# High parts of the MLP weights in a float32 encoder made by a converting GpSimd transfer instead of a ScalarE copy

## The chip, the cores and the metric

The kernel runs on one core of a Trainium2 chip. Its engines are PE (TensorE, the matmuls), PEld (the loads of weights into TensorE), DVE (VectorE), ACT (ScalarE), POOL (GpSimd) and SP (SyncE, which here only issues transfers). The metric is the device time of one execution in microseconds. Lower is better.

## The reference

An encoder of two layers runs over 512 tokens of width 1024. Layer 0 mixes tokens by 2-D neighbourhood attention, layer 1 by sliding-window attention, and each is followed by the same squared-ReLU MLP. Everything is float32.

```python
def squared_relu_mlp(h, w_in, w_out):
    u = jnp.square(jax.nn.relu(jnp.einsum('bsd,df->bsf', h, w_in)))
    return jnp.einsum('bsf,fd->bsd', u, w_out)

def reference(x, mix_norm, mlp_norm, final_norm, na_w_qkv, na_rpb, na_w_o,
              swa_w_qkv, swa_sinks, swa_w_o, t5_rel_table, mlp_w_in, mlp_w_out):
    for i in range(DEPTH):
        j = i // N_MIXERS
        h = rms_norm(x, mix_norm[i])
        if i % N_MIXERS == 0:
            x = x + neighbourhood_attention(h, na_w_qkv[j], na_rpb[j], na_w_o[j])
        else:
            x = x + sliding_window_gqa(h, swa_w_qkv[j], swa_sinks[j], t5_rel_table, swa_w_o[j])
        h = rms_norm(x, mlp_norm[i])
        x = x + squared_relu_mlp(h, mlp_w_in[i], mlp_w_out[i])
    return rms_norm(x, final_norm)
```

`D_MODEL` is 1024, the hidden width `D_FF` is 4096, and both MLPs are of this size.

## The kernel before

**Two parts for each number.** TensorE multiplies in the format float32r, which keeps fewer bits than float32. So every operand is split into a high part (the value rounded to float32r) and a low part (the value less its high part, rounded likewise). One product of float32 tiles is then three matmuls (L364 to L366): high by high, high by low and low by high, all added up in PSUM.

**Weights as a stream of chunks.** The host lays all weights out as 180 chunks of 128x1024 float32, 512 KB each. A chunk is eight 128x128 blocks and so 24 matmuls. Chunks 32 to 95 belong to the first MLP and 116 to 179 to the second. In each MLP the hidden width is done in two halves. A half has 16 chunks of `w_in` (the "hidden" loop, one chunk for each tile of 128 hidden features) and then 16 of `w_out` (the "down" loop, two chunks for each of the 8 output tiles).

**A ring of two.** `w_raw`, `w_hi` and `w_lo` each hold two chunks, even ones in slot 0 and odd ones in slot 1. A chunk `c` passes through four hands:

1. SP loads `w_raw` (L248) once the subtraction of chunk `c-2` is done (`w_split`).
2. ACT copies `w_raw` to `w_hi`, which rounds it (L721). It waits for PE to be done with chunk `c-2` (`w_used`), since that one's high part is in the same slot, and for the load.
3. DVE subtracts, `w_lo = w_raw - w_hi` (L967), and raises `w_split`.
4. PE waits for `w_split`, does the 24 matmuls and raises `w_used`.

Nothing schedules this. Each engine has a program written out in order, and only semaphores couple them. In the hidden loop, PE's end of chunk `f` lets DVE scale the result out of PSUM (`scale_tile`, L995) and then subtract for chunk `f+2`. ACT squares (L753) and rounds (L757) the scaled tile, and DVE makes its low part (`tile_low`, L1005). In the down loop DVE adds the result to the residual `x` (`add_to_x`, L1107) between two subtractions.

**GpSimd** builds the attention biases: it issues the transfers of bias rows (L292, L314) and adds a mask (L304). During the MLPs it has nothing to do.

**The last output tile** (`last_group`) goes through chunks 178 and 179 twice, once for each half of the tokens, so its first pass over chunk 178 takes half as long as that of another chunk.

Of the kernel before, what the change touches and what calls it, by code (L numbers as in the profile page):

```python
# [32 lines left out]
HALF = FF // 2 // P  # L33
# [20 lines left out]
CH_NA, CH_NAO, CH_MLP0 = 0, 24, 32  # L54
CH_SW, CH_SWO, CH_MLP1 = 96, 108, 116
CHUNKS = 180
GR_NA, GR_NAO, GR_MLP0, GR_SW, GR_SWO, GR_MLP1 = 0, 24, 32, 80, 92, 100


# [39 lines left out]
def encoder(nc, xT, wstream, gains, rpb, sinks, rel_table, na_mask, onehot, out):  # L99
# [3 lines left out]
    with ExitStack() as ctx:  # L103
# [56 lines left out]
        t5_product, t5_cleared, t5_made = sem("t5_product"), sem("t5_cleared"), sem("t5_made")  # L160
        nsink_made = sem("nsink_made")

        w_hi_made, w_split, w_used = sem("w_hi_made"), sem("w_split"), sem("w_used")

        acc_taken = sem("acc_taken")
# [108 lines left out]
        @block.gpsimd  # L274
        def _(pool):
            nc.gpsimd.memset(rpb_pad[:], 0.0).then_inc(pool_filled, 1)
            nc.gpsimd.memset(ident[:], 0.0).then_inc(pool_filled, 1)
            pool.wait_ge(pool_filled, 2)
            nc.gpsimd.affine_select(out=ident[:], in_=ident[:], compare_op=ALU.not_equal, fill=1.0, base=0,
                                    pattern=[[-1, P]], channel_multiplier=1).then_inc(ident_made, 1)  # L280
            pool.dma_start(mask[:], na_mask).then_inc(consts_landed, 16)
            pool.wait_ge(rpb_landed, 16)
            for c in range(1, QC, 2):
                pool.dma_start(rpb_dram[c], rpb_pad[:, :, QC - 1 - c:QC - 1 - c + BIASC]).then_inc(rpb_stored_odd, 16)

            def load_na_bias(pair):

                heads = bass.ds((pair * 2).v, 2)
                if pair.a >= 2 or pair.b:
                    pool.wait_ge(bias_made, (pair * 2 + -2).v)  # L290
                for r in range(ROWS):
                    pool.dma_start(bias[QC * r:QC * (r + 1), pair.odd, :, :],  # L292
                                   rpb_dram[:, heads, ROWS - 1 - r:RPB_R - r, :].rearrange("c h r u -> c h (r u)")
                                   ).then_inc(na_bias_landed[pair.odd], 16)

            def masked_bias(pair, g):

                if g == 0:
                    pool.wait_ge(na_bias_landed[pair.odd], ((pair.half + 1) * (16 * ROWS)).v)
                if pair.a >= 1 or pair.b:  # L300
                    pool.wait_ge(logits_made, (pair * 2 + (g - 1)).v)
                for i in range(4):
                    rows, j = bias[:, pair.odd, i // 2, :].rearrange("p (r u) -> p r u", u=BIASC), 2 * g + i % 2
                    ins = nc.gpsimd.tensor_tensor(bias_m[:, g, i, :, :].rearrange("p c r -> p r c"),  # L304
                                                  rows[:, :, U0[j]:U0[j] + WC],
                                                  mask[:, j:j + 1, :].to_broadcast([P, ROWS, WC]), ALU.add)
                ins.then_inc(bias_made, 1)

            def load_t5_bias(pair):

                heads = bass.ds((pair * 2).v, 2)
                for a in range(P // QC):
                    at = P - QC - QC * a
                    pool.dma_start(bias[QC * a:QC * (a + 1), pair.odd, :, :], t5_dram[:, heads, at:at + BAND]  # L314
                                   ).then_inc(t5_bias_landed[pair.odd], 16)

            def place_sinks(pair):

                heads = bass.ds((pair * 2).v, 2)
                nc.gpsimd.tensor_copy(sw_sink[:, pair.odd, :], sink[:, heads])  # L320
                nc.gpsimd.tensor_copy(sw_nsink[:, pair.odd, :], nsink[:, heads]).then_inc(sinks_placed, 1)

            pool.wait_ge(rpb_stored, 16 * QC // 2)
            pool.wait_ge(rpb_stored_odd, 16 * QC // 2)
            load_na_bias(At(0))
            load_na_bias(At(1))
            pool.dma_start(sink[:], sinks.partition_broadcast(P)).then_inc(consts_landed, 16)
            pool.dma_start(table[:], rel_table).then_inc(table_landed, 16)
            pool.dma_start(onehot_sb[:], onehot).then_inc(table_landed, 16)
            pool.wait_ge(consts_landed, 16 * 2)  # L330
            masked_bias(At(0), 0)
            masked_bias(At(0), 1)
            with pool.Fori(0, PAIRS // 2 - 1) as i:
                for n in range(1, 3):
                    pair = At(n, 2, i)
                    load_na_bias(pair + 1)
                    masked_bias(pair, 0)
                    masked_bias(pair, 1)
            masked_bias(At(PAIRS - 1), 0)
            masked_bias(At(PAIRS - 1), 1)  # L340

            pool.wait_ge(t5_made, 1)
            for q in range(QC):
                pool.dma_start(t5_dram[q], t5_row[:, QC - 1 - q:QC - 1 - q + T5_W]).then_inc(t5_stored, 16)
            pool.wait_ge(bias_made, HEADS)
            pool.wait_ge(t5_stored, 16 * QC)
            pool.wait_ge(nsink_made, 1)
            for pair in range(2):
                load_t5_bias(At(pair))
                place_sinks(At(pair))  # L350
            with pool.Fori(1, PAIRS // 2) as i:
                for n in range(2):
                    pair = At(n, 2, i)
                    pool.wait_ge(probs_made, (pair * 4 + (UNITS_NA - 4)).v)
                    pool.wait_ge(esink_made, (pair * 2 + -2).v)
                    load_t5_bias(pair)
                    place_sinks(pair)


        @block.tensor  # L360
# [354 lines left out]
        def _(act):  # L715
# [123 lines left out]
            def mlp(ch, gr, ti, sq, norm):  # L839
                for half in range(2):  # L840
                    c0, g0 = ch + 32 * half, gr + 24 * half
                    if half == 0:
                        deviation(norm)
                    split_weights(At(c0 + 2))

                    def hidden(n, i, first=False):
                        f = At(n, 2, i) if i is not None else At(n)
                        if not first:
                            split_weights(f + (c0 + 2))
                        tile_high(f + g0, f + (ti + HALF * half), u_hi[:, f.v, :], f + (sq + HALF * half))  # L850

                    hidden(0, None, True)
                    hidden(1, None)
                    with act.Fori(1, HALF // 2) as i:
                        hidden(0, i)
                        hidden(1, i)

                    def down(n, i):
                        m = At(n, 2, i) if i is not None else At(n)
                        g = m + (g0 + HALF)  # L860
                        c = m * 2 + (c0 + HALF + 2)
                        if c.a < CHUNKS:
                            split_weights(c)
                        if half == 1:
                            prepare_x(norm + 1, m, lambda: act.wait_ge(acc_taken, (g + 1).v))
                        if (c + 1).a < CHUNKS:
                            split_weights(c + 1)

                    with act.Fori(0, KT // 2 - 1) as i:
                        down(0, i)  # L870
                        down(1, i)
                    down(KT - 2, None)
                    if norm == 3 and half == 1:
                        last_squares()
                        return
                    down(KT - 1, None)
                load_sqrt()
# [85 lines left out]
        @block.vector  # L963
        def _(dve):
            def split_weights(c):
                dve.wait_ge(w_hi_made, (c + 1).v)
                nc.vector.tensor_tensor(w_lo[:, c.odd, :], w_raw[:, c.odd, :], f32(w_hi[:, c.odd, :]),  # L967
                                        ALU.subtract).then_inc(w_split, 1)

# [197 lines left out]
            def mlp(ch, gr, ti, norm):  # L1167
                for half in range(2):
# [3 lines left out]
                    with dve.Fori(0, HALF // 2) as i:  # L1172
                        for n in range(2):
                            f = At(n, 2, i)
                            e = f + (ti + HALF * half)
                            scale_tile(f + c0, f + g0, e, 0.0, ALU.max)
                            split_weights(f + (c0 + 2))
                            tile_low(e, u_lo[:, f.v, :], u_hi[:, f.v, :])
                    if half == 1:
                        clear_squares(norm + 1)  # L1180
# [1 line left out]
                    def down(n, i):  # L1182
                        m = At(n, 2, i) if i is not None else At(n)
                        c = m * 2 + (c0 + HALF)
                        if (c + 2).a < CHUNKS:
                            split_weights(c + 2)
                        add_to_x(c + 1, m + (g0 + HALF), m)
                        if half == 1:
                            finish_x(norm + 1, m)
                        if (c + 3).a < CHUNKS:  # L1190
                            split_weights(c + 3)

                    with dve.Fori(0, KT // 2 - 1) as i:
                        down(0, i)
# [222 lines left out]
```

## Time and profile before

| | |
|---|---|
| median of 3 runs | 1183.13 us (1181.47 to 1183.34) |
| profiled execution, span from first to last instruction | 1181.5 us |
| PE busy | 1148.9 us, 97% |
| PEld busy | 948.7 us, 80% |
| DVE busy | 624.0 us, 53% |
| ACT busy | 467.1 us, 40% |
| POOL busy | 130.1 us, 11% |
| `w_hi` copies on ACT (L721) | 180, 188.9 us in all |
| `w_lo` subtractions on DVE (L967) | 180, 221.4 us in all |
| chain that ended last | 90% PE, 4% DVE |

The profile gives the span of its execution, and no other time of that execution. The span lies at the lower end of the runs. An engine's busy time says how much work it has, not whether anybody waits for it. The chain that ended last is followed back from the last instruction to whatever released each step.

### The profile page before, as it was taken

What the parts mean: (1) busy time and instruction counts of PE and PEld (TensorE: products, weight loads), DVE (VectorE), ACT (ScalarE), POOL (GpSimd) and SP (SyncE); (2) the same over time, 40 slices, a digit from 0 to 9 for tenths busy, and PEclk for the clock granted to TensorE, in tenths of its full rate; (3) what the DMA queues carried; (4) which work ended last, traced back from release to release, by engine and by line L of the source; (5) the groups of instructions that cost most, each with busy time, mean ns of one, the idle gap of its engine ahead of it and who ended that gap; (6) DMA issues with size and microseconds to landing.
All of it is one profiled execution on the core that took longest, in us unless ns stands there. A gap on an engine that the chain in (4) does not pass through costs nothing.

```text
span 1181.5 us, 16835 instructions
## 1 busy us (share of the span) xinstructions
PE 1148.9 (97%) x5770; PEld 948.7 (80%) x5770; DVE 624.0 (53%) x988; ACT 467.1 (40%) x811; POOL 130.1 (11%) x243
## 2 busy tenths in 40 slices
PE   6899999999999999999999999999999999999996
PEld 4788888887888888888887777787888888888886
DVE  7576767575543224453445777766544223454334
ACT  6444545344432123342323655645434122343221
POOL 4734342050000000000000123100000000000000
PEclk9999999999999999999999999999999999999999
DMA  7322222143232222323222122122232222323222
GB/s 207 109 80 72 72 79 66 59 116 107 89 106 90 98 97 89 106 89 106 83 96 89 50 63 62 32 72 88 90 106 90 96 100 90 106 89 106 90 89 90
DMA packets 36851, 106.74 MB, mean 90 GB/s; under 512 B 8225, under 2 KB 10545, under 8 KB 36817
## 3 DMA queue, kind: packets, MB, share of 16 engines
q1 hardware_dynamic: 31680, 98.98, 25.0%
q0 software_dynamic: 4992, 7.29, 2.7%
q8 instruction: 21, 0.34, 0.1%
q14 instruction: 14, 0.11, 0.0%
q10 hardware_dynamic: 144, 0.02, 0.0%
HBM read 102.92 MB, written 3.34 MB: 90 GB/s over the span
## 4 chain that ended last, share of the span: by engine, by line
PE 90%; DVE 4%; issue 1%; SPq 1%; POOL 1%; ACT 1%; DMA 1%; DVEq 0%; ACTq 0%; POOLq 0%
PE acc L364 26%; PE acc L366 25%; PE acc L365 25%; PE s_ps L436 3%; PE o_ps L469 2%; PE o_ps L466 2%; PE pt_ps L457 1%; PE pt_ps L626 1%; SPq L262 1%; DVE w_lo L967 1%; PE misc_ps L469 1%; PE misc_ps L426 1%; POOL bias_pairs L292 1%; PE s_ps L364 1%; PE misc_ps L466 1%
## 5 line engine op out<-in xcount | busy, mean ns | idle before, releaser
L721 ACT CAST w_hi<-w_raw 128x1024 fp32r<-128x1024 f32 x180 | 188.9, 1049 | 416.3 <-PE acc L366 412.5
L364 PE MATMUL acc<-h_hi,w_hi 128*128 128x512 f32 x800 | 324.0, 405 | 10.6 <-DVE sqsum L984 10.1
L366 PE MATMUL acc<-h_hi,w_lo 128*128 128x512 f32 x800 | 313.3, 392 | 0.0
L365 PE MATMUL acc<-h_lo,w_hi 128*128 128x512 f32 x800 | 312.9, 391 | 0.0
L967 DVE TENSOR_TENSOR w_lo<-w_raw,w_hi 128x1024 fp32r<-128x1024 f32 x180 | 221.4, 1230 | 153.0 <-ACT w_hi L721 152.8
L364 PE MATMUL acc<-u_hi,w_hi 128*128 128x512 f32 (+1 forms) x624 | 241.8, 387 | 0.9 <-DVE w_lo L967 0.9
L366 PE MATMUL acc<-u_hi,w_lo 128*128 128x512 f32 (+1 forms) x624 | 239.8, 384 | 0.0
L365 PE MATMUL acc<-u_lo,w_hi 128*128 128x512 f32 (+1 forms) x624 | 239.7, 384 | 0.0
L364 PEld LDWEIGHTS acc<-h_hi,w_hi 128*128 128x128 f32 x800 | 150.7, 188 | 48.5 <-issue 13.9
L366 PEld LDWEIGHTS acc<-h_hi,w_lo 128*128 128x128 f32 x800 | 150.7, 188 | 32.4
L365 PEld LDWEIGHTS acc<-h_lo,w_hi 128*128 128x128 f32 x800 | 151.2, 189 | 28.7 <-issue 1.0
L995 DVE SCALAR_TENSOR_TENSOR scaled<-acc,rstd 128x512 f32<-128x512 f32 x90 | 62.2, 691 | 162.1 <-PE acc L366 161.4
L364 PEld LDWEIGHTS acc<-u_hi,w_hi 128*128 128x128 f32 x624 | 117.3, 188 | 25.9 <-DVE w_lo L967 2.4
L366 PEld LDWEIGHTS acc<-u_hi,w_lo 128*128 128x128 f32 x624 | 117.3, 188 | 23.2
L365 PEld LDWEIGHTS acc<-u_lo,w_hi 128*128 128x128 f32 x624 | 117.4, 188 | 22.4
L765 ACT ACTIVATE probs<-probs,nmax 128x256 f32<-128x256 f32 (+1 forms) x128 | 67.8, 531 | 67.7 <-DVE nmax L1055 67.7
L314 POOL DMA_DIRECT2D bias_pairs<-t_shifted x64 | 32.2, 505 | 471.0 <-ACT esink L895 463.3
L1107 DVE TENSOR_TENSOR x_res<-acc,x_res 128x512 f32 (+1 forms) x39 | 26.9, 691 | 101.1 <-PE acc L366 101.1
L1005 DVE TENSOR_TENSOR u_lo<-scaled,u_hi 128x512 f32 (+1 forms) x80 | 55.3, 691 | 12.5 <-ACT u_hi L757 12.2
L304 POOL TENSOR_TENSOR bias_masked<-bias_pairs,mask 128x256 f32<-128x256 f32 x64 | 45.3, 748 | 91.8 <-DVE nmax L1055 89.4
L1015 DVE TENSOR_TENSOR pt_lo<-pt_ps,pt_hi 128x1024 fp32r<-128x1024 f32 (+2 forms) x48 | 45.8, 954 | 15.6 <-ACT pt_hi L770 15.6
L757 ACT CAST u_hi<-scaled 128x512 f32 (+1 forms) x80 | 49.6, 621 | 10.3 <-DVE scaled L995 3.1
(105 smaller groups left out, 989.3 us busy)
## 6 DMA issues: line engine op xcount, KB each, us to landing
w_raw<-in_wstream SPq DMA_DIRECT2D x180, 512.0 KB, 3.2
bias_pairs<-rpb_shifted POOLq DMA_DIRECT2D x64, 48.0 KB, 3.0
bias_pairs<-t_shifted POOLq DMA_DIRECT2D x64, 48.0 KB, 2.1
x_res<-in_xT SPq DMA_DIRECT2D x8, 256.0 KB, 4.6
out_y<-x_res SPq DMA_DIRECT2D x16, 128.0 KB, 1.8
t_shifted<-vT POOLq DMA_DIRECT2D x16, 31.0 KB, 1.9
rpb_shifted<-rpb_pad POOLq DMA_DIRECT2D x8, 45.0 KB, 5.3
rpb_shifted<-rpb_pad SPq DMA_DIRECT2D x8, 45.0 KB, 8.5
```

The lines of the kernel that those rows point to most:

```text
L304: ins = nc.gpsimd.tensor_tensor(bias_m[:, g, i, :, :].rearrange("p c r -> p r c"), rows[:, :, U0[j]:U0[j] + WC], mask[:, j:j + 1, :].to_br ...
L364: nc.tensor.matmul(dst, a[0], b[0], start=start, stop=False)
L365: nc.tensor.matmul(dst, a[0], b[1], start=False, stop=False)
L366: return nc.tensor.matmul(dst, a[1], b[0], start=False, stop=stop)
L436: ins = nc.tensor.matmul(dst(hh), a[s, queries[0], queries[1]], b[s, keys[0], keys[1]], start=start, stop=stop)
L721: nc.scalar.copy(w_hi[:, c.odd, :], w_raw[:, c.odd, :]).then_inc(w_hi_made, 1)
L757: nc.scalar.copy(dst, src).then_inc(tile_hi, 1)
L765: return nc.scalar.activation(src, src, ACT.Exp, bias=nmax[:, slot, i:i + 1], scale=-1.0, accum_out=rsum[:, slot, i:i + 1])
L967: nc.vector.tensor_tensor(w_lo[:, c.odd, :], w_raw[:, c.odd, :], f32(w_hi[:, c.odd, :]), ALU.subtract).then_inc(w_split, 1)
L995: nc.vector.scalar_tensor_tensor(out=dst, in0=order(acc[g.odd][:]), scalar=factor, in1=order(rstd[:]), op0=op, op1=ALU.mult).then_inc(acc_ ...
L1005: nc.vector.tensor_tensor(order[0](dst), order[1](scaled[:, e.odd, :]), order[0](f32(hi)), ALU.subtract).then_inc(tile_split, 1)
L1015: nc.vector.tensor_tensor(pt_lo[:, 0:blocks, :], pt_ps[:, 0:blocks, :], f32(pt_hi[:, 0:blocks, :]), ALU.subtract).then_inc(pt_split, 1)
```

## The change

In the two MLP stages the high part is no longer made by ACT. GpSimd issues a second transfer of the same chunk out of `wstream`, into `w_hi`, whose type is float32r while the source is float32, so that the transfer converts. It is done for chunks 34 to 97 and 118 to 179, which is 126 of the 180. SP's load of `w_raw` stays as it is, and DVE's subtraction stays, but now waits for both transfers. The semaphore `w_hi_made` counts the remaining copies of ACT.

```diff
+CAST = [(CH_MLP0 + 2, CH_MLP0 + 66), (CH_MLP1 + 2, CHUNKS)]
+CAST_BEFORE = CAST[0][1] - CAST[0][0]
...
+        w_hi_cast = [sem("w_hi_cast0"), sem("w_hi_cast1")]
...
+            def cast_weights(start, stop):
+
+                with pool.Fori(start // 2, stop // 2) as i:
+                    for n in range(2):
+                        c = At(n, 2, i)
+                        pool.wait_ge(w_used, (c + -1).v)
+                        pool.dma_start(w_hi[:, c.odd, :], wstream[c.v]).then_inc(w_hi_cast[c.odd], 16)
+
...
+            cast_weights(*CAST[0])
             with pool.Fori(1, PAIRS // 2) as i:
...
                     place_sinks(pair)
+            cast_weights(*CAST[1])
...
-                    split_weights(At(c0 + 2))
-
-                    def hidden(n, i, first=False):
+
+                    def hidden(n, i):
                         f = At(n, 2, i) if i is not None else At(n)
-                        if not first:
-                            split_weights(f + (c0 + 2))
                         tile_high(f + g0, f + (ti + HALF * half), u_hi[:, f.v, :], f + (sq + HALF * half))
...
                         g = m + (g0 + HALF)
-                        c = m * 2 + (c0 + HALF + 2)
-                        if c.a < CHUNKS:
-                            split_weights(c)
                         if half == 1:
                             prepare_x(norm + 1, m, lambda: act.wait_ge(acc_taken, (g + 1).v))
-                        if (c + 1).a < CHUNKS:
-                            split_weights(c + 1)
...
             def split_weights(c):
-                dve.wait_ge(w_hi_made, (c + 1).v)
+                if c.a < CAST[0][0]:
+                    dve.wait_ge(w_hi_made, (c + 1).v)
+                else:
+                    dve.wait_ge(w_hi_made, (c + (1 - CAST_BEFORE)).v)
+                low_weights(c)
+
+            def split_cast_weights(c, n):
+
+                before = CAST[n][0] // 2 - n * CAST_BEFORE // 2
+                dve.wait_ge(w_landed[c.odd], ((c.half + 1) * 16).v)
+                dve.wait_ge(w_hi_cast[c.odd], ((c.half + (1 - before)) * 16).v)
+                low_weights(c)
+
+            def low_weights(c):
                 nc.vector.tensor_tensor(w_lo[:, c.odd, :], w_raw[:, c.odd, :], f32(w_hi[:, c.odd, :]),
                                         ALU.subtract).then_inc(w_split, 1)
...
                             scale_tile(f + c0, f + g0, e, 0.0, ALU.max)
-                            split_weights(f + (c0 + 2))
+                            split_cast_weights(f + (c0 + 2), norm // 2)
                             tile_low(e, u_lo[:, f.v, :], u_hi[:, f.v, :])
```

The calls of `split_weights` in DVE's down loop are replaced in the same way.

These are ACT's rows for one turn of the hidden loop, two tiles, in the kernel before:

```order
L720 ISA [waits w_used]
L721 CAST w_hi<-w_raw 128x1024 [waits w_landed0]
L753 ACTIVATE scaled<-scaled 128x512 [waits acc_taken]
L754 REGISTER_ALU
L757 ISA [waits squared]
L757 COPY u_hi<-scaled 128x512
L719 REGISTER_ALU
L721 CAST w_hi<-w_raw 128x1024 [waits w_landed1,w_used]
L753 ACTIVATE scaled<-scaled 128x512 [waits acc_taken]
```

Both rows L721 are gone in the changed kernel, and nothing takes their place on ACT. These are GpSimd's rows in the changed kernel, between the first two pairs of bias loads (which end at L332) and the loop over the other pairs:

```order
L332 COPY sw_nsink<-nsink 128x2
L322 UNCONDITIONAL_BRANCH
L322 ISA
L326 ISA [waits w_used]
L326 DMA w_hi<-in_wstream 128x1024
L326 ISA [waits w_used]
L326 DMA w_hi<-in_wstream 128x1024
L322 REGISTER_ALU
L322 COMPARE_AND_BRANCH
L363 UNCONDITIONAL_BRANCH
```

In the kernel before, the branch into the loop over the pairs follows the copy directly. Now a loop of transfers stands between them, each behind a wait of its own, and the same loop stands again at the end of GpSimd's program.

## Rows read from the trace of the kernel before

**Rows 1.** The page's busy times: us, share of the span, instructions.

```profile
PE 1148.9 (97%) x5770; PEld 948.7 (80%) x5770; DVE 624.0 (53%) x988; ACT 467.1 (40%) x811; POOL 130.1 (11%) x243
```

**Rows 2.** Busy time in windows of the MLPs: PE, PEld, DVE, ACT, POOL, clock, DMA share, GB/s.

```profile
284.00:600.00 316.00, 316.00 (x1396) 261.51 (x1395) 130.35 (x145) 102.73 (x131) 0.00 (x0) 1.00 0.28 95
806.00:1157.00 351.00, 350.28 (x1543) 289.27 (x1542) 148.06 (x163) 114.30 (x145) 0.00 (x0) 1.00 0.28 96
```

**Rows 3.** PE's waits from 806 us to the end: us in total, times, longest.

```profile
PE pt_ps L577 <- ACT probs L832: 1.0, 1, 1.0
PE acc L364 <- DVE w_lo L967: 0.7, 2, 0.5
```

**Rows 4.** Timeline of one turn of the hidden loop: start, duration, engine, instruction.

```profile
299.98 0.39 PE L366 MATMUL acc<-h_hi,w_lo 128*128 128x512 f32 x1
300.21 0.39 PE L364 MATMUL acc<-h_hi,w_hi 128*128 128x512 f32 x1
300.41 1.05 ACT L721 CAST w_hi<-w_raw 128x1024 fp32r<-128x1024 f32 x1 [3.03 <-PE acc L366]
301.49 1.23 DVE L967 TENSOR_TENSOR w_lo<-w_raw,w_hi 128x1024 fp32r<-128x1024 f32 x1 [0.39 <-ACT w_hi L721]
302.89 0.33 SPq L248 DMA_DIRECT2D w_raw<-in_wstream  x1
305.42 0.19 PEld L364 LDWEIGHTS acc<-h_hi,w_hi 128*128 128x128 f32 x1
305.65 0.39 PE L364 MATMUL acc<-h_hi,w_hi 128*128 128x512 f32 x1
```

**Rows 5.** Landing of the loads of `w_raw` issued from 300 to 345 us.

```profile
DMA to landing us min/median/max: 3.1/3.3/3.8
```

**Rows 6.** The load issued at 302.89, in windows; columns as in rows 2.

```profile
303.00:303.75 0.75, 0.75 (x5) 0.63 (x4) 0.58 (x1) 0.00 (x0) 0.00 (x0) 1.00 0.00 0
303.75:305.25 1.50, 1.50 (x9) 1.23 (x8) 0.00 (x0) 0.00 (x0) 0.00 (x0) 1.00 0.90 292
305.25:306.00 0.75, 0.75 (x5) 0.63 (x4) 0.15 (x1) 0.07 (x1) 0.00 (x0) 1.00 0.29 115
```

**Rows 7.** Transfers of GpSimd with no load beside them: timeline, then windows.

```profile
662.19 4.16 POOL L314 DMA_DIRECT2D bias_pairs<-t_shifted  x7 [405.70 <-ACT esink L895]
...
662.19:663.19 1.00, 1.00 (x9) 0.83 (x7) 0.74 (x3) 0.43 (x2) 0.88 (x2) 1.00 0.00 0
663.19:664.00 0.81, 0.81 (x10) 0.81 (x9) 0.17 (x3) 0.64 (x3) 0.63 (x2) 1.00 0.34 65
```

**Rows 8.** GpSimd's transfers and their landing: line, count, KB each, median us.

```profile
w_raw<-in_wstream SPq DMA_DIRECT2D x180, 512.0 KB, 3.2
...
bias_pairs<-t_shifted POOLq DMA_DIRECT2D x64, 48.0 KB, 2.1
```

**Rows 9.** The two loads of `w_raw` beside 16 transfers of GpSimd, 246 to 253 us.

```profile
246.87 4.01 POOL L314 DMA_DIRECT2D bias_pairs<-t_shifted  x8 [1.91 <-issue]
...
DMA to landing us min/median/max: 3.4/3.6/3.8
```

**Rows 10.** DMA queues: packets, MB, share of 16 engines over the span.

```profile
q1 hardware_dynamic: 31680, 98.98, 25.0%
q0 software_dynamic: 4992, 7.29, 2.7%
```

**Rows 11.** Timeline of the last group: chunk 177 ends, chunk 179 begins.

```profile
1158.09 0.39 PE L366 MATMUL acc<-u_hi,w_lo 128*128 128x512 f32 x1
1160.84 1.22 DVE L967 TENSOR_TENSOR w_lo<-w_raw,w_hi 128x1024 fp32r<-128x1024 f32 x1 [0.25 <-ACT w_hi L721]
1162.12 0.39 PE L364 MATMUL acc<-u_hi,w_hi 128*128 128x256 f32 x1
```

More of the change, by code:

```diff
@@ L843, in mlp @@
                         deviation(norm)
-                    split_weights(At(c0 + 2))
-                    def hidden(n, i, first=False):
+                    def hidden(n, i):
                         f = At(n, 2, i) if i is not None else At(n)
-                        if not first:
-                            split_weights(f + (c0 + 2))
                         tile_high(f + g0, f + (ti + HALF * half), u_hi[:, f.v, :], f + (sq + HALF * half))
-                    hidden(0, None, True)
+                    hidden(0, None)
                     hidden(1, None)
@@ L1185, in down @@
                         if (c + 2).a < CHUNKS:
-                            split_weights(c + 2)
+                            split_cast_weights(c + 2, norm // 2)
                         add_to_x(c + 1, m + (g0 + HALF), m)
@@ L1190, in down @@
                         if (c + 3).a < CHUNKS:
-                            split_weights(c + 3)
+                            split_cast_weights(c + 3, norm // 2)
                     with dve.Fori(0, KT // 2 - 1) as i:
```

## The prediction

> **What bounds the kernel now.** I read the page's busy times first: PE has work for 1148.9 of the 1181.5 us of the span, and DVE, the next after TensorE's own weight loads, for 53% [rows 1]. The windows over the two MLPs, where the change acts, say more. PE is busy for 316.00 of 316 us in the first and for 350.28 of 351 in the second, at a granted clock of 1.00 [rows 2]. PE's list of waits from 806 us to the end holds 1.7 us in two rows [rows 3]. So in these stages only PE's own work counts. ACT's copies lie wholly beside it, and taking them away from ACT cannot shorten anything by more than those 1.7 us. The question is whether the new way of making `w_hi` still fits into the time that PE leaves it.
>
> That time is read from one turn of the hidden loop [rows 4]. The first matmul of a chunk starts at 300.21 and that of the next at 305.65, so a chunk takes 5.44 us. The last matmul of the chunk before ends at 299.98 + 0.39 = 300.37, and that is when the slot of the chunk after the next is free. ACT starts its copy 0.04 us later, DVE subtracts from 301.49 to 302.72, and PE first reads the result at 305.42 (the weight load). The preparation takes 2.35 us of about 5.05, and 2.7 us are to spare.
>
> **The change part by part.** ACT loses 126 copies of 1.05 us, some 132 us of busy time. They end no wait of PE, so this is worth 0.
>
> The new path from a freed slot to PE is a sum. GpSimd sees the semaphore, taken as 0.05 us like ACT's 0.04. Then come the landing time L of the transfer, 0.10 for DVE to see it, 1.23 for the subtraction [rows 4], and 0.45 to the first matmul counted from the old chunk's last end: 0.06 for the semaphore, 0.23 from weight load to matmul (305.42 to 305.65), and 0.16 by which a chunk's first matmul starts ahead of the end of the last one (300.21 against 300.37). That is G = L + 1.83. PE starts chunk k+2 at the later of two times: its own end of k+1, or G after its end of k. If G is under 5.44, nothing changes, and this asks for L under 3.61. If G is more, two steps of the ring take G + 5.44, so each chunk takes (G + 5.44) / 2 and loses (L - 3.61) / 2. An overshoot is paid half because the ring has two slots.
>
> So everything hangs on L, which no row shows: GpSimd's transfers here move 48 KB, and none goes to a float32r tile. It is built from three pieces:
>
> - Start. SP's load issued at 302.89 moves nothing up to 303.75, that is 0.86 us [rows 4, 6]. GpSimd's issued at 662.19 moves nothing up to 663.19 and begins right after; I take 1.03 [rows 7].
> - Movement. The 16 engines are busy for 0.90 x 1.50 + 0.29 x 0.75 = 1.57 us for 512 KB [rows 6].
> - Landing. SP's median is 3.3 [rows 5], so 3.3 - 0.86 - 1.57 = 0.87 remain. The same pieces put GpSimd's 48 KB at 1.03 + 0.15 + 0.87 = 2.05, where the row has 2.1 [rows 8].
>
> Alone, then, L = 1.03 + 1.57 + 0.87 = 3.47, just under 3.61. But it is not alone. SP issues the next load of `w_raw` when a subtraction ends, 0.17 us after it in the row (302.72 to 302.89). Now the subtraction ends shortly before PE starts the next chunk, which is the moment when GpSimd issues its next transfer. With L = 3.47 the subtraction ends at 0.05 + 3.47 + 0.10 + 1.23 = 4.85 after the slot was freed, and the load moves its bytes from 4.85 + 0.17 + 0.86 = 5.88 to about 7.5. GpSimd's next, issued at 5.49, moves its own from 6.52 to 8.1. They overlap by a microsecond, and if PE waits, still more: the subtraction's end and the freed slot move together. Two transfers that start together take 2 x 1.57, so L = 1.03 + 3.14 + 0.87 = 5.04. The trace has a mild case: beside 16 transfers of 48 KB two loads of `w_raw` took 3.4 and 3.8 us instead of 3.3 [rows 5, 9]. I take the full 5.04, since both issues hang on the same event.
>
> The Trainium skill says this as a rule (DMA: Bandwidth & Descriptors, "Issuing engines are not separate DMA queues"): transfers issued from different engines run on the same 16 DMA engines and interleave, and a second issuer saves only issue time. The mild case above agrees. By this rule the full sharing stands; without it the sum would be near 0.
>
> The loss is then (5.04 - 3.61) / 2 = 0.715 us for each chunk. 126 chunks are made this way, and 125 of them by this pattern: 89.4 us.
>
> Chunk 179 is apart. PE goes through chunk 178 at half length, so 179 is wanted early: chunk 177 ends at 1158.48, the subtraction ends at 1162.06 and PE starts at 1162.12 [rows 11]. The transfer of 179 has no further load beside it, so the subtraction would end at 1158.48 + 0.05 + 3.47 + 0.10 + 1.23 = 1163.33, 1.3 us late.
>
> The other queues move little. SP's order is unchanged. GpSimd did nothing for 405.70 us before its loop over the pairs [rows 7] and nothing at all in the MLP windows [rows 2], and the casts of the first MLP end before that loop's first wait can be met, so no bias is late. DVE now stands in a wait of 4 us or more with `tile_low` behind it, but `tile_low` has until the down loop, and the next `scale_tile` needs the next chunk's end, which comes later: 0. The register work of 252 waits and issues lies in GpSimd's idle time.
>
> The sum is 1181.5 + 89.4 + 1.3 = 1272.2 us against the span of the profiled execution. That execution stands 1.6 us under the median of 1183.13, and I leave it there: **1272 us, 7.5% slower**.
>
> **Bounds of L.** Below: the sharing may be partial, as in the mild case, where 0.5 us were added. L = 4.0 gives 0.2 us a chunk, 25 us and 1208. Above: the conversion. Its nearest row is the software queue as a whole, which took 2.7% of the engines for 7.29 MB against 25.0% for 98.98 MB, 1.47 times as long for each byte (its packets are smaller) [rows 10]. If a converting packet takes 1.47 times a plain one, the shared movement is 1.57 x 2.47 = 3.88, L = 5.78, and the loss 1.085 x 125 = 136: 1318. If it takes twice as long, L = 1.03 + 4.71 + 0.87 = 6.61, 1.5 us a chunk and 188 in all: 1370. I keep the plain rate for the value, because the bytes on both sides are the same.
>
> **The rivals.**
>
> 1. *Hidden anyway, no change.* The transfer's fixed parts are shorter than mine, or the two transfers fall out of step. The point from which it decides is L = 3.61, and then only the tail of 1.3 us is left: 1183. For it: alone L is 3.47 by rows. Against it: the overlap follows from the order of the events, and 0.14 us of margin does not survive it. The Trainium skill's fit for one GpSimd transfer (DMA: Bandwidth & Descriptors, "Anatomy of one DMA — SWDGE (gpsimd) path"), 2.0 us plus bytes over 436 GB/s, gives 3.2 for 512 KB as an estimate and would put the kernel here. No run here shows it for this size. Chance 0.05.
> 2. *Slower than before, but by conversion.* The DMA engines pass converted data at half the rate or less: 1370 and up. For it: nothing in the trace converts, so nothing bounds it. Against it: the same bytes go in and come out. Everything above 1345 gets 0.13.
> 3. *Faster.* ACT's copies no longer stand ahead of `prepare_x` and the squares, so the last group's sums of squares come sooner, and the 1.7 us of waits [rows 3] go: 1180. Against it is the tail term, which is as large. Chance 0.02.
> 4. *The transfer does not convert.* Then `w_hi` is the raw chunk. Time would be as in the forecast, since the bytes and waits are the same. It takes no share of its own. The Trainium skill has it that a float32r destination always casts (DMA: Bandwidth & Descriptors, "SWDGE vs HWDGE vs iDMA"); no row here shows it.
>
> **How the numbers follow.** The forecast case, both transfers sharing the engines at between the plain rate and about 1.7 times it, holds 0.80 and reaches from 1208 to 1345. Those ends leave out rival 2 (0.13) and rivals 1 and 3 (0.07), 2 in 10. I round the lower end to 1205. The three chances come from the same cases, with 0.2% (2.4 us) as about what a measurement of this kernel can tell: faster 0.02, same 0.04, slower 0.94; a fifth of rival 1 ends over the bound.
>
> **What would show it.** In the MLP windows PE is busy for about 88% (5.44 / 6.15), the DMA share is near 0.5 and some 170 GB/s are moved. PE's list of waits has one new large row, for `w_lo`, of some 90 us. DVE's subtraction waits for a DMA, not ACT. The transfers into `w_hi` land after 5.0 us, and those into `w_raw` after 4.7 to 4.9 instead of 3.3. One chunk takes 6.15 us. Outside the MLPs nothing moves. Wrong would be: L near 3.5 with the loads unshifted (the sharing failed), L over 6 (the conversion is priced too low), or a granted clock under 1.00 where PE gets gaps: the MLPs ran at 1.00 without gaps [rows 2], and no row shows them with one in every chunk.

## The result, and the profile after

The changed kernel takes 1276.67 us in the median of 4 runs (1275.56 to 1278.5), the kernel before 1183.0 us. The ratio is 1.0793, with a 95% interval of 1.078 to 1.0807. The forecast was 1272 us, with a range of 1205 to 1345.

The page of the changed kernel, first its busy times:

```profile
PE 1181.3 (93%) x5770; PEld 941.2 (74%) x5770; DVE 611.7 (48%) x988; ACT 342.6 (27%) x685; POOL 197.4 (15%) x369
```

ACT lost 124.5 of its 467.1 us [rows 1], and the span grew by 95.3. The windows over the two MLPs (columns as in [rows 2]):

```profile
284.00:650.00 366.00, 335.13 (x1423) 263.13 (x1421) 126.39 (x148) 45.09 (x72) 31.28 (x59) 1.00 0.51 169
870.00:1250.00 380.00, 350.81 (x1472) 271.59 (x1471) 130.56 (x148) 46.24 (x74) 32.38 (x61) 1.00 0.49 168
```

PE was busy for all of these stages, and now for 92%. The DMA share went from 0.28 to 0.50, the traffic from 95 to 168 GB/s, and the granted clock stayed at 1.00. Then PE's largest waits (us in total, times, longest), and the landing of the two transfers (line, count, KB, median us):

```profile
PE acc L377 <- DVE w_lo L985: 64.3, 101, 2.2
PE acc L377 <- DVE sqsum L1002: 9.6, 2, 8.2
...
w_raw<-in_wstream SPq DMA_DIRECT2D x180, 512.0 KB, 3.4
w_hi<-in_wstream POOLq DMA_DIRECT2D x126, 512.0 KB, 4.6
```

The new wait is the one for `w_lo`. It sums to less than the loss, because PE's busy time grew too, by 32.4 us for the same 5770 instructions [rows 1]. A gap costs more than its idle time: the matmul behind it is drawn with 0.49 instead of 0.39 us, and the 0.16 us by which a chunk's first matmul otherwise starts before the last one ends [rows 4] are gone. Over 101 gaps that is 26 us. What ends DVE's wait before the subtraction is no longer ACT but the transfer:

```profile
DVE w_lo L985 <- DMA w_hi<-in_wstream: 475.7, 122, 6.5
```

One turn of the ring in the changed kernel, in the timeline (start, duration, engine, instruction):

```profile
413.27 0.39 PE L379 MATMUL acc<-u_hi,w_lo 128*128 128x512 f32 x1
413.54 1.23 DVE L985 TENSOR_TENSOR w_lo<-w_raw,w_hi 128x1024 fp32r<-128x1024 f32 x1 [5.90 <-DMA w_hi<-in_wstream]
414.30 0.53 POOL L326 DMA_DIRECT2D w_hi<-in_wstream  x1 [4.91 <-PE acc L379]
414.90 0.49 PE L377 MATMUL acc<-u_hi,w_hi 128*128 128x512 f32 x1 [1.25 <-DVE w_lo L985]
414.94 5.11 SPq L251 DMA_DIRECT2D w_raw<-in_wstream  x2
418.33 1.22 DVE L985 TENSOR_TENSOR w_lo<-w_raw,w_hi 128x1024 fp32r<-128x1024 f32 x1 [2.96 <-DMA w_hi<-in_wstream]
```

A chunk ends at 413.66, and PE stands still for 1.25 us, since the other slot's low part is done only at 414.77. GpSimd's transfer into the freed slot is issued at 414.30, SP's load at 414.94, right behind the end of the subtraction, and the next subtraction can start at 418.33. In [rows 4] the freed slot was ready 2.35 us after the chunk's end. Here it is ready after 5.9 (418.33 + 1.22 - 413.66), while the other slot's chunk lasts PE only 5.57 (the next one starts at 420.47), and 5.44 without a gap before it.

### The profile page after: what moved, and what is told of

It is laid out like the page before. It is cut to its first block, busy times and chain, and to the rows that moved or that the text cites. A ratio compares the mean times of both kernels' runs of the same rounds, so it can differ in the third digit from the quotient of the medians.

```text
span 1276.8 us, 17144 instructions
## 1 busy us (share of the span) xinstructions
PE 1181.3 (93%) x5770; PEld 941.2 (74%) x5770; DVE 611.7 (48%) x988; ACT 342.6 (27%) x685; POOL 197.4 (15%) x369
## 3 DMA queue, kind: packets, MB, share of 16 engines
q1 hardware_dynamic: 31680, 98.98, 23.1%
## 4 chain that ended last, share of the span: by engine, by line
PE 61%; DMA 22%; DVE 9%; issue 5%; POOL 1%; SPq 1%; ACT 1%; POOLq 0%; DVEq 0%; ACTq 0%
DMA w_hi<-in_wstream 21%; PE acc L377 17%; PE acc L379 15%; PE acc L378 15%; DVE w_lo L985 6%; PE s_ps L449 3%; PE o_ps L482 2%; PE o_ps L479 2%; PE pt_ps L470 1%; PE pt_ps L639 1%; SPq L265 1%; PE misc_ps L482 1%; PE misc_ps L439 1%; POOL bias_pairs L295 1%; PE s_ps L377 1%
## 5 line engine op out<-in xcount | busy, mean ns | idle before, releaser
L377 PE MATMUL acc<-h_hi,w_hi 128*128 128x512 f32 x800 | 329.9, 412 | 40.4 <-DVE w_lo L985 29.9
L377 PE MATMUL acc<-u_hi,w_hi 128*128 128x512 f32 (+1 forms) x624 | 247.6, 397 | 35.1 <-DVE w_lo L985 34.3
L326 POOL DMA_DIRECT2D w_hi<-in_wstream x126 | 66.9, 531 | 792.8 <-PE acc L379 701.6
L766 ACT ACTIVATE scaled<-scaled 128x512 f32<-128x512 f32 x64 | 40.5, 632 | 499.9 <-DVE scaled L1013 499.9
L734 ACT CAST w_hi<-w_raw 128x1024 fp32r<-128x1024 f32 x54 | 56.4, 1044 | 50.2 <-PE acc L379 46.4
L744 ACT ACTIVATE h_hi<-x_res,gain 128x512 fp32r<-128x512 f32 (+1 forms) x32 | 23.1, 722 | 117.0 <-DVE x_res L1125 108.9
```

What stands on the lines that cost most here:

```text
L326: pool.dma_start(w_hi[:, c.odd, :], wstream[c.v]).then_inc(w_hi_cast[c.odd], 16)
L377: nc.tensor.matmul(dst, a[0], b[0], start=start, stop=False)
L734: nc.scalar.copy(w_hi[:, c.odd, :], w_raw[:, c.odd, :]).then_inc(w_hi_made, 1)
L766: nc.scalar.activation(src, src, ACT.Square).then_inc(squared, 1)
```

## The experiments

Eleven kernels were run. Five of them keep ACT's copies and send the second transfer into a spare tile that nobody reads; in four of the five GpSimd issues it, in one ACT. So what the transfer costs is seen apart from what ACT's relief gives.

**A plain transfer in the converting one's place.** The edit to the kernel before:

```diff
+        w_spare = sb("w_spare", [P, 2, CHUNK], F32)
...
+                        pool.wait_ge(w_used, (c + -1).v)
+                        pool.dma_start(w_spare[:, c.odd, :], wstream[c.v]).then_inc(w_hi_cast[c.odd], 16)
...
+            def split_late(c, n):
+
+                before = CAST[n][0] // 2 - n * CAST_BEFORE // 2
+                dve.wait_ge(w_hi_cast[c.odd], ((c.half + (1 - before)) * 16).v)
+                split_weights(c)
```

> The kernel before (ACT still makes the high parts), plus GpSimd's second transfer of each of the 126 chunks, plain, into a spare float32 tile that nobody reads but for whose landing DVE's subtraction waits. So it has the new path without its conversion. My theory (the path is start, movement shared with SP's load, landing; conversion costs nothing): 1270 to 1280 us, as the changed kernel with 1276.7, and the transfers land after 4.6 us. Rival (converting packets are slow and make a good part of the 4.6 us): clearly faster than the changed kernel, 1240 or less, landing under 4.2 us.

Measured: 1286.11 us (ratio 1.0875, interval 1.0858 to 1.0893), landing 4.6 us. The rival is out: without any conversion the transfer lands just as late. The time came 6 us over my range. The kernel after the next one bears on that.

**The same with conversion.** The spare tile is `F32R`, and nothing else differs.

> As the plain transfer into a spare tile, but the spare tile is float32r, so that the transfer converts, and ACT still makes the high parts. It differs from the changed kernel only by ACT's 126 copies. My theory: 1277 us within 3 us, since ACT's copies end no wait of TensorE. Rival (freeing ACT gave something back that hid part of the loss): slower than the changed kernel by 5 us or more.

Measured: 1287.33 us (1.0881, 1.086 to 1.0902), not to be told from the plain one. The queue rows of the two (plain first) bound the price of converting:

```profile
q0 software_dynamic: 23136, 73.36, 17.4%
```

```profile
q0 software_dynamic: 23136, 73.36, 18.2%
```

That is 223 against 234 us of the 16 engines (share by the spans of 1284.4 and 1286.5), or 0.09 us for each of the 126 transfers. This is an upper bound: SP's loads, which convert nothing, also took some 4 us more of the 16 engines in the second of these runs (their queue has 23.1% and 23.4%). Both stood 10 us above the changed kernel. Taken as written, my expectation failed and its rival held: freeing ACT seemed to give back 10 us. One more kernel was made for that.

**The two waits in another order.** In the kernel just told, DVE waits for the transfer, computes the value of its wait for ACT's copy, waits again and subtracts. Here the transfer comes last:

```diff
-                dve.wait_ge(w_hi_cast[c.odd], ((c.half + (1 - before)) * 16).v)
-                split_weights(c)
+                dve.wait_ge(w_hi_made, (c + 1).v)
+                dve.wait_ge(w_hi_cast[c.odd], ((c.half + (1 - before)) * 16).v)
+                nc.vector.tensor_tensor(w_lo[:, c.odd, :], w_raw[:, c.odd, :], f32(w_hi[:, c.odd, :]),
+                                        ALU.subtract).then_inc(w_split, 1)
```

> The converting transfer into a spare tile with ACT's copies kept, but DVE waits first for ACT's copy and last for the transfer, as in the changed kernel, so that no register work and no second wait stand between the landing and the subtraction. The first form of this kernel was 10 us slower than the changed one. Theory A (that was the second wait after the landing, some 0.15 us of the path, half charged, 125 times): 1275 to 1280 us. Theory B (ACT's copies themselves cost those 10 us): 1285 to 1290 us.

Measured: 1268.94 us (1.0727, 1.0702 to 1.0752). So ACT's copies are not what cost the 10 us: with all of them in place this kernel is 8 us faster than the changed one. Why it is faster was not found. Exchanging the two waits took off 18 us, which is more than theory A asked, and its 1275 was missed by 6. Little of it stands where theory A put it. By the traces' landings, the subtraction starts 0.10 us after the landing in the mean with the waits as before and 0.06 with them exchanged. Half of 0.04 us, 125 times, is 2.5 us. The rest goes with the landing itself: a median of 4.3 us here against 4.6 in the changed kernel and 4.7 with the waits the other way round. The end of the subtraction lets SP's load go, so a shift there moves the load against the next transfer. How so small a shift comes to change the landing by 0.4 us was not separated.

**ACT's relief alone.** The kernel before, with ACT copying 8 of the 1024 columns in the two stages, so that the high parts of those weights are left out. ACT's other calls of `split_weights` in the two stages are replaced like the one shown.

```diff
+            def touch_weights(c):
+
+                act.wait_ge(w_used, (c + -1).v)
+                act.wait_ge(w_landed[c.odd], ((c.half + 1) * 16).v)
+                nc.scalar.copy(w_hi[:, c.odd, 0:8], w_raw[:, c.odd, 0:8]).then_inc(w_hi_made, 1)
...
-                    split_weights(At(c0 + 2))
+                    touch_weights(At(c0 + 2))
```

> The kernel before, but in the two MLP stages ACT copies only 8 of the 1024 columns of a chunk, so the high parts of those weights are left out. It has the gain of the change without its cost. My theory: at most the 1.7 us of waits in the second stage can go, 1180 to 1183 us. Rival (ACT's copies cost TensorE time that its list of waits doesn't show): 1175 us or less.

Measured: 1182.98 us (1.0001, 0.9992 to 1.001). The gain of the change is 0, as [rows 2] say. Its windows over a stretch of each MLP:

```profile
300.00:600.00 300.00, 300.00 (x1325) 248.13 (x1324) 119.66 (x137) 51.85 (x122) 0.00 (x0) 1.00 0.29 95
900.00:1130.00 230.00, 230.00 (x1017) 190.44 (x1016) 85.32 (x96) 33.02 (x82) 0.00 (x0) 1.00 0.29 96
```

**The traffic without the wait.** The converting transfer into the spare tile, but DVE doesn't wait for it. GpSimd alone does, before it fills the same slot again.

> As the converting transfer into a spare tile, at the same moments, but nobody except GpSimd itself waits for it. It has the traffic of the changed kernel without its wait. My theory: 1182 to 1184 us, no change, since SP's load has more than 3 us to spare. Rival (170 GB/s of traffic into the tiles slows the engines or the matmuls themselves): 1200 us or more.

Measured: 1182.83 us (0.9997, 0.9988 to 1.0006). Its windows and its transfers:

```profile
300.00:600.00 300.00, 300.00 (x1325) 248.07 (x1324) 122.47 (x136) 95.84 (x121) 29.05 (x55) 1.00 0.63 192
...
w_spare<-in_wstream POOLq DMA_DIRECT2D x55, 512.0 KB, 3.6
w_raw<-in_wstream SPq DMA_DIRECT2D x55, 512.0 KB, 4.3
```

192 GB/s go through, more than in the changed kernel, and PE has no gap. The traffic alone costs nothing here, so the whole loss is the wait. Here GpSimd's transfer comes first and SP's load behind it, and now it is the load that lands late (4.3 instead of 3.3 us). It can afford to.

**Another issuer.** ACT issues the plain transfer, ahead of its own copy:

```diff
+            def load_and_split(c):
+
+                act.wait_ge(w_used, (c + -1).v)
+                act.dma_start(w_spare[:, c.odd, :], wstream[c.v]).then_inc(w_hi_cast[c.odd], 16)
+                split_weights(c)
```

> As the plain transfer into a spare float32 tile, but ACT issues it, ahead of its own copy of the same chunk, instead of GpSimd. The trace of the changed kernel shows GpSimd's issue 0.6 us after the end of the chunk that it waits for, where I had 0.05. My theory with that term: without it and with SP's start of 0.86 us the path is about 0.7 us shorter, half of it is saved for each chunk, and the time is 1225 to 1240 us. Rival (the issuer makes no difference, only the shared engines do): 1265 us or more.

Measured: 1240.13 us (1.0477, 1.0447 to 1.0506), at the upper end of what was expected. Of its timeline, with the end of a chunk first:

```profile
407.86 0.39 PE L370 MATMUL acc<-u_hi,w_lo 128*128 128x512 f32 x1
408.40 0.69 DVE L1123 TENSOR_TENSOR x_res<-acc,x_res 128x512 f32 x1 [1.46 <-PE acc L370]
408.42 0.34 ACTq L730 DMA_DIRECT2D w_spare<-in_wstream  x1
412.67 1.23 DVE L977 TENSOR_TENSOR w_lo<-w_raw,w_hi 128x1024 fp32r<-128x1024 f32 x1 [3.58 <-DMA w_spare<-in_wstream]
```

The chunk ends at 408.25, and ACT issues 0.17 us later, which is also the median of its 126 issues. GpSimd's issue stood 0.64 us after the chunk's end. Against the plain transfer from GpSimd this saves 46 us, 0.37 for each chunk, and by the rule of half that is a path shorter by 0.74. The starts differ by 0.47 (issue) and 0.17 (first byte, 1.03 less 0.86 [rows 6, 7]), 0.64 together. The agreement is rough, for the landing fell by more than the first byte, from a median of 4.6 to 3.7 us. So the run shows that the issuer matters, and not how much of it is the issue and how much the landing.

**Loads let go by the landing.** In the changed kernel, GpSimd lets SP's load go once the converting transfer of the chunk before has landed (and the subtraction that still reads the load's slot is done):

```diff
+                        pool.wait_ge(w_hi_cast[c.odd], ((c.half + (1 - before)) * 16).v)
+                        pool.wait_ge(w_split, c.v)
+                        pool.sem_inc(w_go, 1)
```

> The changed kernel, but SP's load of a chunk in the two stages is let go by GpSimd, once the converting transfer of the chunk before has landed. So the two transfers no longer overlap. My theory (sharing adds 1.1 us to the landing): the transfer lands after 3.4 to 3.6 us, the path from freed slot to TensorE is 0.6 + 3.45 + 1.78 = 5.83 us, the loss for each chunk 0.2 us, and the time 1200 to 1212 us. Rival (the landing is as long by itself, through conversion or a slow start): it stays at 1270 us or more.

Measured: 1257.12 us (1.0595, 1.0544 to 1.0646), and a landing of 4.3 us in the median, 3.4 to 5.9. My number was 45 us off. Two turns tell why: SP's issue, then GpSimd's issue and the subtraction that waits for it.

```profile
393.79 0.33 SPq L254 DMA_DIRECT2D w_raw<-in_wstream  x1
395.38 0.53 POOL L331 DMA_DIRECT2D w_hi<-in_wstream  x1 [5.67 <-DVE w_lo L993]
399.85 1.23 DVE L993 TENSOR_TENSOR w_lo<-w_raw,w_hi 128x1024 fp32r<-128x1024 f32 x1 [4.99 <-DMA w_hi<-in_wstream]
```

```profile
412.10 0.33 SPq L254 DMA_DIRECT2D w_raw<-in_wstream  x1
414.15 0.53 POOL L331 DMA_DIRECT2D w_hi<-in_wstream  x1 [6.03 <-PE acc L387]
417.74 1.23 DVE L993 TENSOR_TENSOR w_lo<-w_raw,w_hi 128x1024 fp32r<-128x1024 f32 x1 [3.38 <-DMA w_hi<-in_wstream]
```

In the first turn the load goes out 1.59 us ahead of the transfer, and the transfer lands after 4.45. In the second it goes out 2.05 ahead, and the landing takes 3.50, no more than in the next run, where no load is near. Over all 126 transfers the median landing is 3.65 us for the 30 whose load was issued at least 1.8 us ahead, and 4.37 for the 88 with 1.0 to 1.8 us. Windows over the end of the first turn's transfer, then over the second's (the last two columns are DMA share and GB/s):

```profile
398.00:398.50 0.50, 0.50 (x4) 0.40 (x3) 0.00 (x0) 0.00 (x0) 0.00 (x0) 1.00 0.69 246
398.50:399.50 1.00, 1.00 (x6) 0.84 (x5) 0.00 (x0) 0.00 (x0) 0.00 (x0) 1.00 0.07 25
...
416.75:417.50 0.75, 0.75 (x5) 0.63 (x4) 0.00 (x0) 0.00 (x0) 0.00 (x0) 1.00 0.50 175
417.50:418.25 0.75, 0.75 (x5) 0.63 (x4) 0.51 (x1) 0.00 (x0) 0.00 (x0) 1.00 0.00 0
```

The second transfer is through 3.35 us after its issue (417.50). The first is nearly through after 3.12 (398.50), but for one more microsecond a DMA share of 0.07 stays busy, about what one engine in 16 makes, and only then does it land. By the trace's packets the load's bytes ended 1.30 us after the transfer's issue and the transfer's began at 1.27, so the two hardly overlapped. In most turns, then, the load came too close, and this run did not set the two apart, which it was made for. The next one does.

**Loads in the middle of a chunk.** TensorE reports when it is through the first four blocks of a chunk, and SP's load waits for that alone:

```diff
+                if mid is not None:
+                    sp.wait_ge(w_half, (c + -mid).v)
...
+                    if half and k == BLOCKS // 2 - 1:
+                        ins.then_inc(w_half, 1)
```

> The changed kernel, but in the two stages SP's load of a chunk is let go when TensorE is through the first four blocks of the chunk before it by two, 2.7 us after a slot is freed. In the run with loads let go by the landing they came about a microsecond later than I had meant and still stood next to the following transfer, so that it landed after 4.4 us. Here they lie in the middle. My theory (the load's neighbourhood makes the landing long): the converting transfer lands after 3.6 us, as where nobody waited for it, the path is 0.6 + 3.6 + 1.78 = 5.98 us, and the time 1210 to 1225 us. Rival (the landing is 4.4 us wherever the load lies, so something of GpSimd's own transfer makes it long): 1250 us or more.

Measured: 1217.7 us (1.0285, 1.026 to 1.031). In its trace SP's load is issued at 407.41 and GpSimd's transfers at 404.80 and 410.58, and they land so (stretch of the first MLP):

```profile
w_raw<-in_wstream SPq DMA_DIRECT2D x53, 512.0 KB, 3.3
w_hi<-in_wstream POOLq DMA_DIRECT2D x53, 512.0 KB, 3.5
```

Moving nothing but the moment of SP's load takes 1.1 us off the landing and 59 us off the time, 63% of the loss. So the load next to it is what lengthens the transfer's landing. How it does so is not shown: the first turn above was late almost without any overlap.

**The transfer in two halves.** With the same report, the first 512 columns are transferred from the middle of the old chunk on, and only the other half waits for its end.

```diff
+                        pool.wait_ge(w_half, (c + -done).v)
+                        pool.dma_start(w_hi[:, c.odd, 0:CHUNK // 2], wstream[c.v][:, 0:CHUNK // 2]
+                                       ).then_inc(w_hi_cast[c.odd], 16)
                         pool.wait_ge(w_used, (c + -1).v)
+                        pool.dma_start(w_hi[:, c.odd, CHUNK // 2:], wstream[c.v][:, CHUNK // 2:]
+                                       ).then_inc(w_hi_cast[c.odd], 16)
```

> The changed kernel, but each chunk's transfer goes in two halves of 512 columns. TensorE reports when it is through the first four blocks of a chunk, and the first half is issued then, 2.7 us early; only the second half, 256 KB, still hangs on the end of the chunk. My theory: the second half lands after 2.7 us alone and about 3.2 us shared, the path is 5.6 us, and the time 1185 to 1200 us. Rival (the fixed part of the transfer and the number of transfers decide, not the bytes): 1240 us or more.

Measured: 1228.9 us (1.0392, 1.0357 to 1.0428), between the two expectations. The second half landed after 3.6 us, where I had 3.2. Then both edits with the loads let go by the landing:

> Both edits together: the transfer in two halves, and SP's loads let go after the landing. My theory: the path is 0.6 + 2.7 + 1.78 = 5.1 us, under the 5.44 us that TensorE takes for a chunk, so the whole loss is gone: 1182 to 1186 us, no faster than the kernel before. Rival (a free ACT is worth something once the wait is gone): under 1178 us.

Measured: 1207.39 us (1.0202, 1.0187 to 1.0217). That is 21 us over what I expected, and the rival is out as well. The second half landed after 3.3 us, where I had 2.7; what the rest is stays open. And halves with the loads in the middle of a chunk:

> The transfer in two halves, and SP's loads let go in the middle of a chunk. My theory: the second half lands after about 2.8 us, the path is 0.6 + 2.8 + 1.78 = 5.2 us, under 5.44, and the time is within 4 us of the kernel before, 1182 to 1187 us, and not under it. Rival (two small transfers have a fixed part of 3.3 us each, as both halves took in the earlier run): 1200 us or more.

Measured: 1197.17 us (1.012, 1.0095 to 1.0144), 10 us over what I expected and just under the rival's range, though not by the rival's reason: the second half landed after 2.9 us and not after 3.3. Four subtractions in a row of its hidden loop:

```profile
330.16 1.23 DVE L996 TENSOR_TENSOR w_lo<-w_raw,w_hi 128x1024 fp32r<-128x1024 f32 x1 [2.80 <-DMA w_hi<-in_wstream]
...
335.64 1.23 DVE L996 TENSOR_TENSOR w_lo<-w_raw,w_hi 128x1024 fp32r<-128x1024 f32 x1 [2.85 <-DMA w_hi<-in_wstream]
...
341.00 1.23 DVE L996 TENSOR_TENSOR w_lo<-w_raw,w_hi 128x1024 fp32r<-128x1024 f32 x1 [2.76 <-DMA w_hi<-in_wstream]
...
346.48 1.22 DVE L996 TENSOR_TENSOR w_lo<-w_raw,w_hi 128x1024 fp32r<-128x1024 f32 x1 [2.80 <-DMA w_hi<-in_wstream]
```

The step is 5.44 us (16.32 over three): there the wait is wholly hidden. PE's wait for `w_lo` is 9.4 us in all, in 8 places, and the largest is this one:

```profile
575.62 0.53 POOL L331 DMA_DIRECT2D w_hi<-in_wstream  x1 [1.91 <-PE acc L388]
...
581.05 0.53 POOL L334 DMA_DIRECT2D w_hi<-in_wstream  x1 [4.90 <-issue]
...
586.58 0.49 PE L386 MATMUL acc<-u_hi,w_hi 128*128 128x512 f32 x1 [3.42 <-DVE w_lo L996]
```

For GpSimd's idle 4.90 us the profile names nobody. The register row that directly precedes this issue stands at 577.8, when its wait was over, and the transfer was issued 3.2 us later, where 0.5 is usual. The same happens at 1138.76, with 3.22 us of PE behind it. It is no accident of one execution: in all three kernels with halves it is the 222nd and the 398th transfer of GpSimd that come 3.2 us after their register row. The two gaps make 6.6 of the 15 us by which this kernel is slower than the one before. Where the rest stands was not traced.

None of these kernels beats the one before, and this road leads no further: PE has no gap in these stages to win back [rows 2].

## Why the prediction was right

**The bound, and ACT's copies at nothing.** Right, and shown twice: without the copies the time is 1.0001 of before, and with the copies kept beside the transfer it is no longer than without them (1268.94).

**The path G and the charge of half.** Right in its sum. With measured terms it is 0.64 (issue after the chunk's end) + 4.6 (landing) + 0.10 + 1.23 + 0.29 (to the first matmul) = 6.86 where I had 6.87. Half of 6.86 - 5.44 is 0.71 us a chunk, 89 us for 125. The longer matmul behind each of 101 gaps, which I had not priced, adds 10, and the tail 1.2: 100 us, where the span grew by 95.3. Halving is an average: the landing varies from 3.3 to 5.2, and gaps of 1.25 us stand beside chunks with none.

**Its terms were off in three places, and that they cancel is luck.** The 0.05 us for GpSimd to see the semaphore, taken over from ACT's row, is 0.64. No row of before shows GpSimd's answer to a wait in this place, and I should have bounded it instead of borrowing. The landing of 5.04 is 4.6. And the 0.45 to the first matmul is 0.29, since a waiting PE does not pay the 0.23 between weight load and matmul in full: it starts 0.13 us after the subtraction (413.54 + 1.23 = 414.77, then 414.90). The three errors are +0.59, -0.44 and -0.16.

**Sharing.** Right that the load beside it lengthens the landing, too large in size. I let the two transfers meet fully, 1.57 us. Setting them apart takes 1.1 us off (4.6 to 3.5), and the 3.5 that is left is my 3.47 for a transfer alone; rival 1 had named 3.2 for it. (There the first byte came 1.24 us after the issue in the median and not 1.03, so here too the pieces cancel.) That the 1.1 us are shared movement, as I reckoned, is not shown: the transfer issued at 395.38 in the run with loads let go by the landing hardly overlapped its neighbour and was late by 0.95. My mild case was weak evidence too, since its longest load of 3.8 us is also the longest of the loads alone [rows 5, 9]. The rule of the Trainium skill that I had weighed (DMA: Bandwidth & Descriptors, "Issuing engines are not separate DMA queues") agrees with what was measured as far as it goes: a load issued by SP delays a transfer issued by GpSimd. It needs a complement here: another 66 MB of traffic cost nothing as long as nobody waited at the wrong moment.

**The conversion at the plain rate.** Right: at most 0.09 us a transfer, and 1286.11 against 1287.33. Rival 2 and the upper bound of 1318 rested on a higher price and are out. Rival 3 (faster) is out with the time itself, and rival 4 forecast the same time as the main case, so no time tells it apart.

**Rival 1, hidden anyway.** Its point of decision was put at L = 3.61. With the issue 0.59 later and the 0.16 at the end it is 3.2 (5.44 - 0.64 - 0.10 - 1.23 - 0.29), so that even a transfer alone misses it. The run with loads apart shows this: 3.5 us of landing, and still 1217.7.

**The tail.** 1.3 us were predicted for chunk 179. The changed kernel's timeline has it at 1.22:

```profile
1256.18 1.23 DVE L985 TENSOR_TENSOR w_lo<-w_raw,w_hi 128x1024 fp32r<-128x1024 f32 x1 [2.07 <-DMA w_hi<-in_wstream]
1257.46 0.39 PE L377 MATMUL acc<-u_hi,w_hi 128*128 128x256 f32 x1 [1.22 <-DVE w_lo L985]
```

**Signs in the profile.** DMA share near 0.5, 168 GB/s for my 170, and the clock at 1.00 came as said. PE's busy share was 92% and not 88%, and its wait row 64 and not 90 us, for the reason given under the result. SP's loads land after 3.4, not 4.7 to 4.9: the load was issued first in 85 of the 126 pairs, and the one behind pays. Outside the MLPs hardly anything moved: from the subtraction for chunk 97 to that for chunk 117 it is 203.8 us before and 202.6 after.

## What to carry to other kernels

Work of an engine that no one waits for was free here, and replacing it by a transfer put 5.2 us (0.64 to the issue, 4.6 to the landing) where a copy of 1.05 us had stood. Before doing so, add up the path from the freed buffer to its next reader and compare it with the time that the other buffer lasts. Where two transfers hang on the same event, move the one with slack to another moment: here that alone gave back 59 of 94 us. And compare the orders of the waits before an instruction by running them: with the one that ends last standing last, this kernel was 18 us faster, though only some 2.5 us of that can be read off the path behind the landing.

## What the runs showed of the hardware

- GpSimd's issue of a transfer stood 0.64 us after the end of the chunk that it waited for, ACT's 0.17 us (medians of 126).
- Converting float32 to float32r in a GpSimd transfer of 512 KB cost at most 0.09 us of the 16 engines' time beside a plain one.
- Of two 512 KB transfers next to each other the later one lands up to 1 us late, even where their bytes hardly overlap. Behind a load issued 1.0 to 1.8 us earlier the median landing was 4.37 us, behind one at least 1.8 us earlier 3.65, and 3.5 with the load in the middle of the chunk. In the late transfer shown above, a DMA share of 0.07 stayed busy for the last microsecond. Why was not found.
- GpSimd's issue came 3.2 us after its register row instead of 0.5 at the 222nd and the 398th of its transfers, in each of the three kernels with halves. Its cause stays open.
